# Part 1 of the second feed-forward product: nine seven-product and nine plain groups a pass, some seven-product groups side by side, and remainders of the first two sums one at a time

## The reference

```
hdn = jnp.square(jax.nn.relu(jnp.einsum('bsd,df->bsf', x, w_ff1[l])))    # 256 x 8192
ff_out = jnp.einsum('bsf,fd->bsd', hdn, w_ff2[l])                        # 256 x 2048
x = layer_norm(DEEPNORM_ALPHA * x + ff_out, ln2_g[l], ln2_b[l])
```

## Time and profile before

| what | us |
|---|---|
| median of three runs | 1088.34 (1088.18 to 1088.39) |
| the profiled execution | 1088.89 |
| its span, first to last instruction | 1087.1 |
| TensorE busy | 1081.4 |
| VectorE busy | 822.6 |
| ScalarE busy | 578.2 |

### The profile page before, as it was taken

The page is one execution under the profiler, slowest core; times in us unless marked ns, Lnnn a source line. Parts: engine busy times, 40 slices in busy tenths (PEclk is TensorE's granted clock), DMA queues, the critical chain, the costliest instruction groups (busy, mean ns, idle before and its releaser), DMA issues.

```text
span 1087.1 us, 13951 instructions
## 1 busy us (share of the span) xinstructions
PE 1081.4 (99%) x5586; PEld 918.4 (84%) x5586; DVE 822.6 (76%) x923; ACT 578.2 (53%) x756; POOL 24.5 (2%) x43
## 2 busy tenths in 40 slices
PE   9999999999999999999999999999999999999998
PEld 7888888888888888888888888888888888888886
DVE  6587758666666685667699999766776678889998
ACT  6487757665544524445465456444454455545461
POOL 1000101010000000000000000000000000000000
PEclk9999999999999999999999999999999999999999
DMA  9857665557545835665656566566656655655862
GB/s 300 263 177 224 185 191 156 175 177 247 176 155 168 285 108 156 192 193 176 218 189 231 169 220 232 167 188 191 191 174 204 219 177 198 228 195 190 282 222 78
DMA packets 108048, 213.84 MB, mean 197 GB/s; under 512 B 6784, under 2 KB 38016, under 8 KB 107472
## 3 DMA queue, kind: packets, MB, share of 16 engines
q1 hardware_dynamic: 107216, 209.61, 60.1%
q0 software_dynamic: 624, 3.21, 1.0%
q10 hardware_dynamic: 144, 0.13, 0.0%
HBM read 210.83 MB, written 2.10 MB: 196 GB/s over the span
## 4 chain that ended last, share of the span: by engine, by line
PE 98%; DVE 1%; DMA 1%; issue 0%; SPq 0%; ACT 0%; DVEq 0%
PE low_ps L802 11%; PE low_ps L639 10%; PE high_ps L802 9%; PE high_ps L824 7%; PE high_ps L823 7%; PE high_ps L822 7%; PE low_ps L531 6%; PE low_ps L527 6%; PE low_ps L529 6%; PE low_ps L808 5%; PE high_ps L808 5%; PE low_ps L644 5%; PE low_ps L823 3%; PE low_ps L824 3%; PE low_ps L822 3%; PE high_ps L576 1%
## 5 line engine op out<-in xcount | busy, mean ns | idle before, releaser
L1333 DVE TENSOR_TENSOR w_lo<-w_raw,w_hi 128x1024 fp32r<-128x1024 f32 x175 | 213.1, 1222 | 133.6 <-ACT w_hi L993 132.2
L993 ACT ACTIVATE w_hi<-w_raw 128x1024 fp32r<-128x1024 f32 x175 | 185.1, 1059 | 188.5 <-PE low_ps L531 69.5
L802 PE MATMUL low_ps<-x1T,w_hi 128*128 128x512 f32 x512 | 177.3, 393 | 0.0
L802 PE MATMUL high_ps<-x1T,w_hi 128*128 128x512 f32 x448 | 155.1, 393 | 0.0
L639 PE MATMUL low_ps<-xT,w_hi 128*128 128x512 f32 x448 | 144.2, 398 | 0.0
L808 PE MATMUL low_ps<-x1T,w_lo 128*128 128x256 f32 x512 | 139.3, 278 | 0.0
L1663 DVE TENSOR_TENSOR w_lo<-w_raw,w_hi 128x1024 fp32r<-128x1024 f32 x72 | 87.0, 1222 | 59.7 <-ACT w_hi L1194 59.7
L1218 ACT ACTIVATE sum_hi<-sum_raw 128x1024 fp32r<-128x1024 f32 x60 | 63.6, 1063 | 124.7 <-DVE sum_raw L1685 112.8
L808 PE MATMUL high_ps<-x1T,w_lo 128*128 128x256 f32 x448 | 122.1, 278 | 0.0
L1194 ACT ACTIVATE w_hi<-w_raw 128x1024 fp32r<-128x1024 f32 x72 | 76.1, 1060 | 86.4 <-PE low_ps L802 43.4
L802 PEld LDWEIGHTS low_ps<-x1T,w_hi 128*128 128x128 f32 x512 | 94.9, 187 | 20.1
(11 more groups left out here) (214 smaller groups left out, 1915.4 us busy)
## 6 DMA issues: line engine op xcount, KB each, us to landing
w_raw<-in_w_ff SPq DMA_DIRECT2D x208, 512.0 KB, 4.3
w_raw<-in_w_in SPq DMA_DIRECT2D x93, 512.0 KB, 4.3
more_raw<-in_w_ff SPq DMA_DIRECT2D x42, 512.0 KB, 5.2
w_raw<-in_w_out SPq DMA_DIRECT2D x32, 512.0 KB, 3.7
x_raw<-in_x_turned SPq DMA_DIRECT2D x8, 256.0 KB, 6.4
y<-in_x SPq DMA_DIRECT2D x8, 256.0 KB, 4.6
side_raw<-in_w_ff SPq DMA_DIRECT2D x4, 512.0 KB, 6.7
w_raw<-in_w_in SPq DMA_DIRECT2D x6, 256.0 KB, 5.8
```

The costliest lines, as they stand in the source:

```text
L802: return pe.matmul(banks[:, b, :], w_hi[:, slot, cols], x1T[:, t, :, :].rearrange("p h t -> p (h t)"), start=(t == 0 and not lows_open), s ...
L993: act.activation(w_hi[:, slot, :], w_raw[:, slot, :], ACT.Copy).then_inc(w_rounded, units)
L1333: dve.tensor_tensor(w_lo[:, slot, :], w_raw[:, slot, :], w_hi[:, slot, :].bitcast(F32), ALU.subtract).then_inc(w_split, units)
```

## The change

- Chunk 15 becomes one of the chunks with a seven-product group (`FAST_CHUNKS`), so that both passes of part 1 have nine of each kind instead of eight and ten. Its hidden part grows by three blocks; some of its remainders are kept in a tile of their own, `hid_end`, in room that is free by then.
- The order of the kinds is written out (`PASS_KINDS`). Part 0's stays as it was, alternating. In part 1's passes two seven-product groups stand side by side at two places each.
- The rounding and the remainder of sums 0 and 1 are done as two pieces of 512 columns instead of one of 1024, so each seven-product group has five of each instead of four, and TensorE waits for the pieces one by one.

```diff
--- before.py
+++ after.py
@@ -67,26 +67,26 @@
 ROPE_AFTER = [CHUNK_END[i] + (2 if i == 2 else 0) for i in ROPE_CHUNK]
 VALUES_AFTER = [CHUNK_END[i] for i in VALUE_CHUNK]
 FF_PARTS = ((0, 7), (7, 16))
-FAST_CHUNKS = range(1, CHUNKS_FF - 1)
-DOUBLE = 1
-FAST_PAIRS = [t for c in FAST_CHUNKS for t in ((TPC * c, TPC * c + 2) if c == DOUBLE else (TPC * c + 2,))]
+FAST_CHUNKS = range(1, CHUNKS_FF)
+DOUBLE = (1,)
+FAST_PAIRS = [t for c in FAST_CHUNKS for t in ((TPC * c, TPC * c + 2) if c in DOUBLE else (TPC * c + 2,))]
 BLOCKS = [2 * TPC + 3 * len([t for t in FAST_PAIRS if t // TPC == c]) for c in range(CHUNKS_FF)]
 HID_AT = [2 * sum(BLOCKS[FF_PARTS[c >= FF_PARTS[0][1]][0]:c]) for c in range(CHUNKS_FF)]
 HALF = D_MODEL // 2
 FF1_PART = UPH * FF_PARTS[0][1]
 
 
+PASS_KINDS = {(0, 0): "fp" * 7, (0, 1): "fp" * 7,
+              (1, 0): "ppfpfpffpfpfpffpfp",
+              (1, 1): "fpfpfpffpfpffpfppp"}
+
+
 def pass_order(part, half):
 
     tiles = [t for c in range(*FF_PARTS[part]) for t in (TPC * c, TPC * c + 2)]
-    fast = [t for t in tiles if t in FAST_PAIRS]
-    opens_plain = (part, half) == (1, 0)
-    plain = [t for t in tiles if t not in fast]
-    order = plain[:2] if opens_plain else []
-    for t, u in zip(fast, plain[len(order):]):
-        order += [(t, True), u]
-    order += [t for t in plain if t not in order]
-    return [t if isinstance(t, tuple) else (t, False) for t in order]
+    fast = iter([t for t in tiles if t in FAST_PAIRS])
+    plain = iter([t for t in tiles if t not in FAST_PAIRS])
+    return [(next(fast if kind == "f" else plain), kind == "f") for kind in PASS_KINDS[part, half]]
 
 
 PASSES = [(part, half) for part in range(2) for half in range(2)]
@@ -101,6 +101,7 @@
 PAIR_SLOT = [(q + 2) % 3 if q < PART_END else (q - PART_END) % 3 for q in range(len(PAIRS) - 1)] + [3]
 PAIR_LAP = [PAIR_SLOT[:q].count(PAIR_SLOT[q]) + 1 for q in range(len(PAIRS))]
 TAIL = 3
+SUM_COLS = [slice(0, NC), slice(NC, 2 * NC), slice(2 * NC, 4 * NC)]
 OWN_COLS = [slice(0, NC), slice(NC, 3 * NC)]
 LAST = len(PAIRS) - 1
 LAST_AFTER = 3
@@ -182,6 +183,7 @@
 
     H0 = X0 + 32 * KB
     hid = at("hid", [P, 97 * KB // 4], F32R, H0)
+    hid_end = at("hid_end", [P, 2 * TPC * P], F32R, X0 + 28 * KB)
     zeros = at("zeros", [P, P], F32, H0)
     ln2_gb = at("ln2_gb", [P, 2, D_MODEL], F32, H0)
     mixT_hi = at("mixT_hi", [P, HEADS, SEQ], F32R, H0)
@@ -336,7 +338,11 @@
         return low_ps if i % 2 else high_ps
 
     def hid_block(c, b, low):
+        if c == CHUNKS_FF - 1 and low and b < 2 * TPC:
+            return hid_end[:, b * P:(b + 1) * P]
         first = (HID_AT[c] + (BLOCKS[c] if low else 0) + b) * P
+        if c == CHUNKS_FF - 1 and low:
+            first -= 2 * TPC * P
         return hid[:, first:first + P]
 
     def hid_part(c, low):
@@ -463,7 +469,7 @@
         if n < FF1_PART + SLOTS:
             last = PART_END - 3 if n < FF1_PART + 2 else PART_END - 2
             if FAST[last]:
-                sp.wait_ge(fast_split, 4 * (NTH[last] + 1))
+                sp.wait_ge(fast_split, 5 * (NTH[last] + 1))
             else:
                 sp.wait_ge(plain_split, 2 * (NTH[last] + 1))
         else:
@@ -488,7 +494,7 @@
         elif q == PART_END + 5:
             sp.wait_ge(w_used, U_FF1 + UPH * CHUNKS_FF)
         elif FAST[q - 3]:
-            sp.wait_ge(fast_split, 4 * (NTH[q - 3] + 1))
+            sp.wait_ge(fast_split, 5 * (NTH[q - 3] + 1))
         else:
             sp.wait_ge(plain_split, 2 * (NTH[q - 3] + 1))
         for n in range(2):
@@ -858,14 +864,15 @@
                 pe.wait_ge(hid_split, c + 1)
             if first:
                 low_free(p)
-            pe.wait_ge(fast_split, 4 * g + 1)
+            pe.wait_ge(fast_split, 5 * g + 1)
             three(low_ps[:, 1, :], c, more + 1, *of_sum(0), first, last)
+            pe.wait_ge(fast_split, 5 * g + 2)
             three(low_ps[:, 2, :], c, more, *of_sum(1), first, last).then_inc(fast_used, 1)
-            pe.wait_ge(fast_split, 4 * g + 2)
+            pe.wait_ge(fast_split, 5 * g + 3)
             three(low_ps[:, 3, :], c, more + 2, *of_sum(2), first, last)
 
             def own_to_low():
-                pe.wait_ge(fast_split, 4 * g + 3)
+                pe.wait_ge(fast_split, 5 * g + 4)
                 ins = three(low_ps[:, 0, :], c, b, *of_own(0), first, last)
                 if last:
                     ins.then_inc(low_done, 1)
@@ -878,7 +885,7 @@
                 high_free(p, 0)
             else:
                 own_to_low()
-            pe.wait_ge(fast_split, 4 * g + 4)
+            pe.wait_ge(fast_split, 5 * g + 5)
             three(high_ps[:, 0, :], c, b + 1, *of_own(1), opens, False)
             three(high_ps[:, 1, :], c, b + 2, *of_own(2), opens, False).then_inc(fast_used, 1)
 
@@ -1212,9 +1219,8 @@
         def round_sums(q):
 
             g = NTH[q]
-            for n in range(2):
-                cols = slice(2 * n * NC, 2 * (n + 1) * NC)
-                act.wait_ge(fast_summed, 3 * g + (1, 3)[n])
+            for cols, summed in zip(SUM_COLS, (1, 1, 3)):
+                act.wait_ge(fast_summed, 3 * g + summed)
                 act.activation(sum_hi[:, cols], sum_raw[:, cols], ACT.Copy).then_inc(fast_rounded, 1)
 
         def round_own(q):
@@ -1653,6 +1659,15 @@
 
         def split_hidden(i):
             dve.wait_ge(hid_rounded, i + 1)
+            if i == CHUNKS_FF - 1:
+                whole, hi = hidden_whole(), hid_part(i, False).bitcast(F32)
+                dve.tensor_tensor(hid_end[:, :].rearrange("p (k x) -> p k x", k=TPC), whole,
+                                  hi[:, 0:2 * TPC * P].rearrange("p (k x) -> p k x", k=TPC), ALU.subtract)
+                first = (HID_AT[i] + BLOCKS[i]) * P
+                dve.tensor_tensor(hid[:, first:first + (BLOCKS[i] - 2 * TPC) * P],
+                                  hidden[:, 2 * TPC:BLOCKS[i], :].rearrange("p b t -> p (b t)"),
+                                  hi[:, 2 * TPC * P:], ALU.subtract).then_inc(hid_split, 1)
+                return
             dve.tensor_tensor(hid_part(i, True), hidden[:, 0:BLOCKS[i], :].rearrange("p b t -> p (b t)"),
                               hid_part(i, False).bitcast(F32), ALU.subtract).then_inc(hid_split, 1)
 
@@ -1698,9 +1713,8 @@
         def split_sums(q):
 
             g = NTH[q]
-            for n in range(2):
-                cols = slice(2 * n * NC, 2 * (n + 1) * NC)
-                dve.wait_ge(fast_rounded, 4 * g + n + 1)
+            for n, cols in enumerate(SUM_COLS):
+                dve.wait_ge(fast_rounded, 5 * g + n + 1)
                 dve.tensor_tensor(sum_lo[:, cols], sum_raw[:, cols], sum_hi[:, cols].bitcast(F32),
                                   ALU.subtract).then_inc(fast_split, 1)
 
@@ -1708,7 +1722,7 @@
 
             g, part = NTH[q], PASSES[PAIRS[q][0]][0]
             for n, cols in enumerate(OWN_COLS):
-                dve.wait_ge(fast_rounded, 4 * g + 3 + n)
+                dve.wait_ge(fast_rounded, 5 * g + 4 + n)
                 dve.tensor_tensor(own_lo[part][:, cols], pair_raw(q)[:, NC:4 * NC][:, cols],
                                   own_hi[part][:, cols].bitcast(F32), ALU.subtract).then_inc(
                                       fast_split, 1)
```

## The result

The change makes the kernel slower: 1094.71 us (median of six, 1094.24 to 1095.19) against 1088.31 us (six, 1088.03 to 1088.41), ratio 1.0059, 95% interval 1.0048 to 1.007. The prediction was 1095.0 us. The profiled execution after has a span of 1093.4 us.

A forecast was written before the change was run, and what follows sets the result against it. TensorE bounds the kernel, VectorE 0.97 us short of setting the end. VectorE's owed 113.27 us from 962.01 start the tail at 1075.28, not 1068.65: 1088.34 + 6.63 = 1095.0 us; range 1090.2 to 1097.6, the forecast's own 1093.5 to 1096.3.

The forecast's parts named there:

- TensorE's saving: In part 1's two passes, one more seven-product group each saves 3 matmuls: 1.36 us in all, the most to be gained.
- A side-by-side pair: Two adjacent seven-product groups in part 1: TensorE loses 0.41 plus 0.42 us, 0.83 us, even where VectorE is otherwise early.
- C8 and C15: Places 8 and 15 in part 1's first pass, each ending a side-by-side pair: TensorE waits about 0.8 us there.
- the two trades: A plain group becomes seven-product once in each part 1 pass: saves TensorE 1.36 us, gives VectorE 8.84 us in all.
- The pieces: First remainder of each seven-product group's sums, 1024 columns as two of 512: 0 us on VectorE, bounds 0 to 0.16.
- Chunk 15's added hidden work: Opening of part 1's first pass: three small operations and a second remainder piece, priced at nothing; some 1.5 us without cover.
- The queue: VectorE's work from its last rest in part 1's first pass, 962.01, to the first tail addition, 1075.28: 113.27 us.
- The waits of TensorE: Part 1, by place (C first pass, D second): about 0.8 to 1.4 us each, together near 7 us less 1.36.
- Transfers: Loads issued three groups ahead, landing in 5.2 to 8.1 us: only landings over some 7.9 us late, none taken.
- Side-by-side losses only: Rival: VectorE catches up between the four pairs of part 1, only 4 x 0.83 us counts: 1090.3 us; chance 0.10.
- VectorE ahead: Rival: VectorE stays ahead through part 1, TensorE's saving alone is left: 1087.0 us; chance 0.04.
- the emptied pipe: Rival: VectorE's pipe empties behind each operation, the split costs 11 x 0.16 = 1.76 us more: 1096.7 us; chance 0.07.

The follow-up runs named there:

- experiment 10: Changed kernel with second remainders of 16 plain groups cut to 8 columns and a second sums' buffer at all four side-by-side pairs: 1087.80 us, ratio 0.9995.
- experiment 3: Kernel before plus the pieces, eight and ten groups, one side-by-side pair in part 1's first pass: 1089.05 us against 1088.20, ratio 1.0008.
- experiment 9: Kernel of experiment 3, with the sums of the pair's second group in another 8 KB buffer: 1088.23 us against 1088.19, ratio 1.0.
- experiment 5: Changed kernel with VectorE relieved, second remainders of 16 plain groups in part 1 cut from 1024 to 8 columns: 1090.60 us, ratio 1.0022.
- experiment 1: Kernel before with only the pieces added, sums 0 and 1 as two pieces of 512 columns: 1088.27 us against 1088.20, ratio 0.9999.
- experiment 2: Changed kernel without the pieces, sums 0 and 1 again as one piece of 1024 columns: 1095.03 us, ratio 1.0063.
- experiment 4: Changed kernel with the second side-by-side pair of part 1's first pass moved earlier: 1092.28 us, ratio 1.0039.
- experiment 7: Changed kernel with only two second remainders cut to 8 columns, early in part 1's second pass: 1094.31 us, ratio 1.0054.
- experiment 8: Changed kernel with only two second remainders cut to 8 columns, late in part 1's second pass: 1092.70 us, ratio 1.0041.
- experiment 12: Changed kernel with second sums' buffer for four pairs and the own blocks' 1024-column remainder in part 1 on GpSimd: 1105.54 us, ratio 1.0159.
- experiment 6: Kernel before with second remainders of plain groups in part 1 cut to 8 columns, as control: 1088.33 us against 1088.26, ratio 1.0002.

## Why the prediction was right

Point by point, by its own steps:

- **TensorE's saving, 1.36 us.** Holds: with both causes taken away (experiment 10) TensorE is 1.10 us ahead, that is 1.36 less the 0.23 that it still loses.
- **A side-by-side pair costs 0.83 us by itself.** Measured 0.78 at C8 and C15, 0.84 in the distance of experiment 3; experiment 9 shows that the single sums' buffer makes it. The sum is better than its parts: 0.41 and 0.42 us were forecast, 0.47 and 0.31 came, and the two errors offset each other in part. Four pairs alone cost more than the two trades save, so this order could not gain even with a free VectorE (experiment 5: 1090.60).
- **The pieces cost VectorE nothing.** Shown by experiment 1, and that they buy 0.1 to 0.2 us a pair and nothing at the end by experiment 2. The section of the Trainium skill that the prediction holds against this zero ("VectorE: DVE Perf Modes", "The DRAIN you can't avoid") also says that a next operation that is not held starts earlier; the prediction left that half out, and with it the page does not speak against the zero. The trace agrees with it: in D7's group the operation at 1016.44 starts 0.61 us after the one at 1015.83, which lasts 0.69.
- **Chunk 15's added hidden work, priced at nothing.** Holds. The three small operations shortened VectorE's rest in front of C3's sums from 2.22 us (before, at 905.42) to 1.10 (at 905.16), and the second remainder piece (0.55 us at 915.35) came out of what is still a rest of 2.97 us at C8.
- **The queue.** VectorE's last rest was forecast at C15, at 962.01, 2.5 us long; it was 2.51 us, ending at 961.78 with C entered 0.27 us earlier. The debt from there to the first tail addition was forecast at 113.27 us and took 1074.95 - 961.78 = 113.17. The shift was forecast at 6.63 us and is 6.57. Experiments 4, 7 and 8 show that it is this ledger, and not a sum of losses, that gives the end: work counts in full behind the last rest and only in part before it.
- **The waits of TensorE.** 1.4 us forecast in D1, 1.37 found; 1.2 or more at D8 and D13, 1.34 and 1.07 found, the second a little less; about 1 in the last three groups, 0.80 found.
- **Transfers.** None late: no wait of TensorE or VectorE in the changed kernel ends with one.
- **The rivals.** Side-by-side losses only (1090.3) is what experiment 5 gives once VectorE is relieved; in the full kernel it falls short by 4.4 us. VectorE ahead, and the emptied pipe, are excluded by the absence of rests and by experiment 1.

The median came out 0.3 us under the forecast; the executions spread over 0.95 us, from 1094.24 to 1095.19.

## What to carry to other kernels

When one engine is 99% busy and a second has 1 us to spare at the point where the tail begins, a trade that takes 0.68 us from the first and gives 4.42 us to the second can be a loss, as here, although the second engine's average share was only 76%. Find the second engine's last rest and add up its list from there: that sum gives the end, and work saved in front of the rest is mostly given back. Two steps that share one buffer and were spaced by a third step can pay, when put side by side, for the part of the buffer's refill that the first step does not cover (0.8 us a pair here); a second buffer (experiment 9), or keeping the third step in between, avoids it.

## What the runs showed of the hardware

GpSimd's subtraction of 1024 columns took 2.57 us, twice VectorE's 1.22, and VectorE's operation beside it stretched to 3.42 us (experiment 12). Cutting 18 of VectorE's operations from 1024 to 8 columns in the kernel before (experiment 6) did not speed TensorE's matmuls: the distance stayed at 175.74 us to the hundredth. TensorE's pauses in the changed kernel, 0.2 to 0.9 us each, left its granted clock at 1.00, the level of 2.4 GHz (the row of 962 to 1075 us); each cost one matmul step of 0.30 to 0.34 instead of 0.23 us besides.
